# State-space stage: GpSimd builds its table of output powers after VectorE's table of input powers

## The reference

```python
def s5_mixer(u, a_re, a_im, log_dt, b_re, b_im, c_re, c_im, d_skip, w_glu):
    ...
    a_bar = jnp.exp(A * dt)
    b_bar = ((a_bar - 1.0) / A)[..., None] * lax.complex(b_re.astype(f32), b_im.astype(f32))
    bu = jnp.einsum('gpc,bsgc->bsgp', b_bar, u.astype(jnp.complex64))
    h = jax.vmap(lambda bu_b: lax.associative_scan(_linear_combine, (a_seq, bu_b), axis=0)[1])(bu)
    y = jnp.einsum('gcp,bsgp->bsgc', c_mat, h).real + d_skip.astype(f32) * u
    y = jax.nn.gelu(y.reshape(b, s, SSM_WIDTH))
    return y * jax.nn.sigmoid(y @ w_glu.astype(f32))
```

## Time and profile before

| | us |
|---|---|
| median of three runs | 3617.27 |
| profiled execution | 3616.54 |
| its span, first to last instruction | 3614.8 |
| TensorE busy | 3448.6 (95%) |
| VectorE busy | 1589.6 (44%) |
| ScalarE busy | 1173.4 (32%) |
| GpSimd busy | 428.5 (12%) |
| mean granted clock of TensorE | 0.965 of full speed |

### The profile page before, as it was taken

One profiled execution on the slowest core, in us unless ns is written; L12 is line 12 of the kernel. 1 busy time (PEld: TensorE's weight loads), 2 busy tenths in 40 slices (PEclk: granted clock), 3 DMA queues, 4 the chain that ended last, 5 costly groups with the idle time before them and its releaser, 6 DMA issues.

```text
span 3614.8 us, 39886 instructions
## 1 busy us (share of the span) xinstructions
PE 3448.6 (95%) x14476; PEld 2616.2 (72%) x14476; DVE 1589.6 (44%) x2287; ACT 1173.4 (32%) x1725; POOL 428.5 (12%) x301
## 2 busy tenths in 40 slices
PE   7999998999999999998899999899999997899998
PEld 5888773678887788775477888566678885568886
DVE  3332587434323433287534332744343326544322
ACT  4322344433222332244334321213333214543222
POOL 1110003111100110001211110401011002111100
PEclk9999998899999999999699999999999998999999
DMA  4332320023333332331013333331123332223332
GB/s 132 95 96 93 82 82 31 1 70 93 93 94 95 90 93 93 93 82 60 1 30 87 93 97 94 93 74 47 47 82 93 93 93 82 59 70 94 97 93 76
DMA packets 420124, 286.04 MB, mean 79 GB/s; under 512 B 57416, under 2 KB 395180, under 8 KB 419884
## 3 DMA queue, kind: packets, MB, share of 16 engines
q1 hardware_dynamic: 419200, 283.62, 27.2%
q10 hardware_dynamic: 828, 1.13, 0.1%
HBM read 280.24 MB, written 4.47 MB: 79 GB/s over the span
## 4 chain that ended last, share of the span: by engine, by line
PE 89%; DVE 6%; ACT 2%; issue 1%; DMA 0%; POOL 0%; DVEq 0%; ACTq 0%; SPq 0%; POOLq 0%
PE bank L848 25%; PE bank L849 25%; PE bank L850 24%; PE bank L1232 1%; PE bank L1115 1%; PE bank L1116 1%; PE bank L1134 1%; PE bank L843 1%; PE bank L1226 1%; PE bank L1349 1%; DVE arena L2021 1%; DVE small L2019 1%; PE bank L946 0%; DVE arena L2192 0%; PE bank L1092 0%
## 5 line engine op out<-in xcount | busy, mean ns | idle before, releaser
L850 PE MATMUL bank<-xn_lo,w_hi 128*128 128x512 f32 x2800 | 1098.7, 392 | 0.0
L848 PE MATMUL bank<-xn_hi,w_hi 128*128 128x512 f32 x2496 | 1002.4, 402 | 53.7 <-DVE xn_lo L1911 20.6
L1922 DVE TENSOR_TENSOR w_lo<-wring,w_hi 128x1024 fp32r<-128x1024 f32 x478 | 594.5, 1245 | 926.1 <-ACT w_hi L1475 925.0
L849 PE MATMUL bank<-xn_hi,w_lo 128*128 128x512 f32 x2496 | 990.8, 397 | 0.0
L1475 ACT ACTIVATE w_hi<-wring 128x1024 fp32r<-128x1024 f32 x490 | 517.7, 1059 | 1211.8 <-DMA wring<-in_ffn_down 357.6
L850 PEld LDWEIGHTS bank<-xn_lo,w_hi 128*128 128x128 f32 x2800 | 529.5, 189 | 132.7
L848 PEld LDWEIGHTS bank<-xn_hi,w_hi 128*128 128x128 f32 x2496 | 471.0, 189 | 177.1 <-issue 61.2
L849 PEld LDWEIGHTS bank<-xn_hi,w_lo 128*128 128x128 f32 x2496 | 471.9, 189 | 104.6 <-issue 2.6
L849 PE MATMUL bank<-h_hi,w_lo 128*128 (+1 forms) x1056 | 421.4, 399 | 0.0
L848 PE MATMUL bank<-h_hi,w_hi 128*128 (+1 forms) x1056 | 416.3, 394 | 0.0
L850 PE MATMUL bank<-h_lo,w_hi 128*128 (+1 forms) x1056 | 414.0, 392 | 0.0
(11 more groups left out here) (375 smaller groups left out, 3046.4 us busy)
## 6 DMA issues: line engine op xcount, KB each, us to landing
wring<-in_ffn_gate SPq DMA_DIRECT2D x88, 512.0 KB, 3.8
wring<-in_ffn_up SPq DMA_DIRECT2D x88, 512.0 KB, 3.8
wring<-in_ffn_down SPq DMA_DIRECT2D x88, 512.0 KB, 3.5
wring<-in_ffn_w_gate SPq DMA_DIRECT2D x44, 512.0 KB, 3.8
wring<-in_ffn_w_up SPq DMA_DIRECT2D x44, 512.0 KB, 3.7
wring<-in_ffn_w_down SPq DMA_DIRECT2D x44, 512.0 KB, 3.5
wring<-in_w_in SPq DMA_DIRECT2D x34, 512.0 KB, 3.7
wring<-in_w_out SPq DMA_DIRECT2D x16, 512.0 KB, 4.0
```

The source lines that it names most:

```text
L848: nc.tensor.matmul(ps, w_hi[:, slot, t, 0:M], hi, start=start, stop=False)
L849: nc.tensor.matmul(ps, w_lo[:, slot, t, 0:M], hi, start=False, stop=False)
L850: return nc.tensor.matmul(ps, w_hi[:, slot, t, 0:M], lo, start=False, stop=stop)
L1922: nc.vector.tensor_tensor(w_lo[:, slot, :, :].rearrange("p k c -> p (k c)"), wunit[:, slot, :], w_hi[:, slot, :, :].rearrange("p k c -> p ...
```

## The change

GpSimd's wait ahead of its table asks for all 12 instructions of VectorE's table (`x_pow` 12) where it asked for the powers alone (`par` 40). No instruction is added, removed or moved on any engine.

```diff
             pool.e.wait_ge(norm_ps.h, 3 * DEPTH + 1)
             G.memset(s5_tm, 0.0).then_inc(t_zero.h, 1)
-            pool.e.wait_ge(par.h, 40)
+            pool.e.wait_ge(x_pow.h, 3 * S5_Q)
             pool.e.wait_ge(cd_sb.h, 2)
             for i in range(S5_Q):
                 gs = slice(GQ * i, GQ * (i + 1))
```

## The result

| | before | changed |
|---|---|---|
| median of 7 runs each | 3610.27 | 3591.38 |
| lowest to highest | 3603.55 to 3617.30 | 3584.96 to 3599.41 |
| profiled execution, span | 3614.8 | 3583.2 |
| mean granted clock | 0.965 | 0.972 |

The ratio is 0.9947, with a 95% interval of 0.9934 to 0.9960, or 19.1 us (14.4 to 23.8) of 3610. Faster was right. The time itself lies 3 us under the predicted range of 3594.5 to 3607.

A forecast was written before the change was run, and what follows sets the result against it. TensorE, busy 95%, was taken as the bound, so only its waits could pay: `v 2` 17.8 us earlier, less 0.8 for the clock, takes 17.0 off 3616.54, giving 3599.5; plus 0.7 for the median, 3600, range 3594.5 to 3607.

The forecast's parts named there:

- the median of the runs lies 0.7 above that execution, so 3600.2: Last step: from the profiled execution's forecast of 3599.5 us to the median of the runs, rounded to 3600.
- VectorE's table alone: VectorE's twelve table multiplies without GpSimd beside them: 14.2 us, ending at 2321.3 instead of 2341.94.
- TensorE up to `v 2`: Both `wv` waits (10.9 us) go; TensorE could start `v 2` at 2362.2, or 2371.5 with the clock low.
- VectorE up to the rotation: VectorE's table, GpSimd's turns and the steps behind sum to 59.6 us; the rotation of quarter 0 ends at 2367.0.
- B: GpSimd holds the shared ports until its table is done; 12.9 us gained, 3604 to 3606; chance 0.13.
- C: VectorE's short steps get most turns and push GpSimd behind; 22.7 us gained, near 3594.5; chance 0.10.
- D: Half given back: VectorE's steps behind the table pay 3.07 us each, or clock and weight block cost; 3607 to 3612; chance 0.12.
- ScalarE's sines: The 5.94 us hold of quarter 0's rotation by ScalarE's sines goes; they are over by 2362.
- Together: `v 2` needs TensorE's arrival and VectorE's rotation; likeliest start 2367.1, 17.8 us earlier than 2384.94.
- The clock after the new wait: TensorE's low clock behind a new wait of up to 4.9 us ahead of `v 2`: 0.8 us lost, bounds 0 and 2.6.
- The size of the gain: Whole kernel: 17.8 us earlier at `v 2` less 0.8 for the clock, 17.0 us, staying until the end.
- Rival E: VectorE's table is slow by its own broadcast inputs, 3.07 us an instruction; slower, 3621 to 3623; chance 0.03.

## Why the prediction was wrong in its number, point by point

**The step that failed** is "the median of the runs lies 0.7 above that execution, so 3600.2", with a range that held no term for it. It took the level of three runs as that of the kernel. Of 54 runs of the kernel before the highest is 3617.63 and their mean 3609.4; the three that I had, 3614.69 to 3617.30, were from the top of a spread of 14 us. They all belong to the upper group, which holds 12 of the 54. From 3609.4 the forecast gain of 17.0 gives 3592.4, against the measured median of 3591.38, and the range moved down by the same 7.8 us, 3586.7 to 3599.2, holds it. Of the 8.8 us between 3600.2 and the result, 7.0 are the level (3617.27 against 3610.27 over seven runs) and 1.9 a gain that was larger than forecast. The trace held a hint: 0.78 and 0.76 over 550 to 700 and 1650 to 1800 us are stretches with many changes between the two levels of the clock, whose sum need not repeat.

**VectorE's table alone** was right: 14.2 us forecast, 14.2 measured.

**TensorE up to `v 2`.** Both waits went. From the start of `wv 0` I gave 42.6 us with the clock up (2362.2 less 2319.56) and 51.9 with it low in `kt` and behind it; it was 47.5, with `kt` at 9.28 (6.9 to 13.5) and the projection at 10.05. That the clock could fall inside `kt`, which the trace of before suggested, was right.

**VectorE up to the rotation.** Turns moved and did not vanish: right, and within 1.8 us. I had 59.9 us from the table's start to the end of line 2376 (2307.12 to 2367.0); it was 58.1 (2294.76 to 2352.88). Rivals B and C fell, and D's 3.07 us a step with them. C got one thing right: line 2307 read 0.19 us and got past GpSimd.

**ScalarE's sines.** Their wait of 5.94 us went, as forecast: line 1726 ended at 2340.99, 11 us before the rotation.

**Together.** `v 2` was forecast 47.5 us after `wv 0` (2367.1 less 2319.56) and came 47.54 after. The agreement is luck. VectorE's way was 1.8 us shorter than forecast, but its table also started only 10.7 us ahead of `wv 0` and not 12.4, because the stage's first projections ran at the full clock; the two cancel. And I named VectorE as the bound: TensorE came to `v 2` without a wait, by its own clock, with VectorE 0.15 us ahead. Relieving TensorE alone brought nothing (47.53 us with `kt` mixed in), and relieving VectorE alone brought no more than TensorE's clock happened to give (45.86, taken back in the tail).

**The clock after the new wait**, 0.8 us, was not there, because the new wait was not. The run with `kt` mixed in had the wait, and there the low clock cost 4.2 us up to `v 3` (2.7 over the whole tail), above my upper bound of 2.6: I had counted the projection alone, but `v 2` (3.65 us for 1.96) and `sv 1` (2.02 for 1.08) ran low as well.

**The size of the gain.** 17.0 us was forecast; the stretch alone gave 17.8 and 18.5 against the two traces of before, and the means of all runs 19.9. The forecast had taken 0.8 off for the clock behind a wait that didn't come. The 1 to 2 us between the stretch and the means are not assigned. The low clock in the first projections, 15.67 against 13.97 us for 32 matmuls, was seen in one of two traces of the kernel before and in some of the variants with the new wait, so I count it to the level, though the four traces of the changed kernel all have 13.97.

**Rival E** fell at once: 1.22 us an instruction.

## What to carry to other kernels

Two engines that take turns, as VectorE and GpSimd did here, gain nothing from running side by side. Let the one go first whose result is awaited, and price the other's turns on whatever stands behind it, since their sum stays. When a wait goes, work out both arrivals at the next meeting point, with the clock low and high. Before a range in microseconds is given, ask how far the level of identical runs moves; where stretches at a changing clock stand ahead of the change, compare a stretch between two fixed instructions, not the span.

## What the runs showed of the hardware that I had not expected

- A 128x1024 memset on GpSimd (0.95 us) runs beside VectorE's two-input instructions without slowing them (1.23 us); a multiply of that size turns them into 3.05.
- The granted clock fell behind a row of 32 weight loads with 16 columns each (3.6 us), though TensorE was booked busy throughout. With the same products in eights between pairs of 128x512 matmuls it stayed full for 33 us, 14 of which were this mix.
- VectorE's scans suffer much: eight of 128x64 took 11.09 and 12.89 us in two runs beside GpSimd's table, 1.57 alone.
- Steps with one SBUF input took turns as well (line 2314: 2.93 us beside GpSimd's table, 1.23 alone). The multiply on line 2376, which takes one input from a PSUM bank and one from SBUF, read 0.69 us beside GpSimd's late table as it does alone.
- Runs of one program differ by 14 us in 3610. Two traces of the kernel before, 6.6 us apart in span, differ in the granted clock of two stretches with many short waits (0.78 and 0.76 against 0.80 and 0.81).
